# One 512-column matmul for both row parts in the second half of the keys, halves added by VectorE

## What is computed

```python
def step(ht):                                   # h: normed rows of the tokens
    q = (ht @ wq).reshape(T, 8, 2, 64)
    v1, i1 = lax.top_k(q[:, :, 0] @ keys1.T, 16)
    v2, i2 = lax.top_k(q[:, :, 1] @ keys2.T, 16)
    cv, ci = lax.top_k(v1[..., :, None] + v2[..., None, :], 16)   # over the 256 sums
    e = a * 128 + b                             # a, b: the two keys of a chosen pair
    g = jax.nn.softmax(cv, axis=-1)
    act = jax.nn.gelu(jnp.einsum('thkd,td->thk', u_tab[e], ht))
    return jnp.einsum('thk,thkd->td', (g * act), v_tab[e])
x = x + step(rms_norm(x, ffn_norm[l]))
```

## Time and profile before

| | |
|---|---|
| median of three runs | 2247.32 us (2244.87 to 2247.33) |
| the profiled execution | 2247.14 us |
| its span, first to last instruction | 2244.7 us |
| TensorE busy | 2190.7 us, 98% |
| weight loads | 1936.3 us, 86% |
| VectorE busy | 1182.9 us, 53% |
| ScalarE busy | 1169.5 us, 52% |
| GpSimd busy | 1742.0 us, 78% |
| mean granted TensorE clock | 0.991 of full speed |
| second half of the keys, layer 1 | from about 540 to 747 us |
| value pieces, layer 1 | from about 751 us on |
| second half of the keys, layer 2 | from about 1652 to 1860 us |

### The profile page before, as it was taken

One profiled execution on the slowest core, in us unless ns is written; L12 is line 12 of the kernel. 1 busy time (PEld: TensorE's weight loads), 2 busy tenths in 40 slices (PEclk: granted clock), 3 DMA queues, 4 the chain that ended last, 5 costly groups with the idle time before them and its releaser, 6 DMA issues.

```text
span 2244.7 us, 51285 instructions
## 1 busy us (share of the span) xinstructions
PE 2190.7 (98%) x15514; PEld 1936.3 (86%) x15514; DVE 1182.9 (53%) x2295; ACT 1169.5 (52%) x2277; POOL 1742.0 (78%) x1316
## 2 busy tenths in 40 slices
PE   7999999999999999999999999999999999999999
PEld 6887879999999888888879777799999998888887
DVE  5645447994343555434356455489744345554333
ACT  5445664555444444555553556645554444545565
POOL 6745957998777788888885567689987777888887
PEclk9999999999999999999998999999999999999999
DMA  7423534555444454465563334345544444545555
GB/s 265 151 94 113 169 114 149 178 168 170 160 165 160 155 166 167 168 210 191 189 242 122 105 121 160 124 158 174 170 162 163 159 164 154 166 167 188 196 188 177
DMA packets 100823, 368.20 MB, mean 164 GB/s; under 512 B 11520, under 2 KB 12032, under 8 KB 100480
## 3 DMA queue, kind: packets, MB, share of 16 engines
q1 hardware_dynamic: 97344, 354.46, 47.4%
q10 hardware_dynamic: 3392, 12.66, 1.5%
HBM read 366.03 MB, written 1.05 MB: 164 GB/s over the span
## 4 chain that ended last, share of the span: by engine, by line
PE 92%; issue 3%; DVE 3%; POOL 1%; ACT 1%; POOLq 0%; DVEq 0%
PE acc L1058 11%; PE acc L1141 11%; PE acc L1143 10%; PE acc L1142 10%; PE acc L1059 10%; PE acc L1060 10%; PE acc L838 6%; PE acc L840 6%; PE acc L839 6%; PE aux L1100 4%; PE aux L800 2%; POOL w_lo L458 1%; PE aux L951 1%; PE aux L974 1%; PE aux L886 1%
## 5 line engine op out<-in xcount | busy, mean ns | idle before, releaser
L458 POOL TENSOR_TENSOR w_lo<-raw,w_hi 128x512 fp32r<-128x512 f32 x1312 | 1741.8, 1342 | 493.1 <-ACT w_hi L489 385.2
L489 ACT ACTIVATE w_hi<-raw 128x512 fp32r<-128x512 f32 x1348 | 845.3, 629 | 807.8 <-PE acc L1060 419.6
L1058 PE MATMUL acc<-h_hi,w_hi 128*128 128x256 f32 x2048 | 587.3, 287 | 10.6 <-POOL w_lo L458 9.6
L1059 PE MATMUL acc<-h_lo,w_hi 128*128 128x256 f32 x2048 | 579.4, 283 | 0.0
L1060 PE MATMUL acc<-h_hi,w_lo 128*128 128x256 f32 x2048 | 579.1, 283 | 0.0
L1141 PE MATMUL acc<-w_hi,eg 128*128 128x512 f32 x1024 | 405.8, 396 | 0.0
L1058 PEld LDWEIGHTS acc<-h_hi,w_hi 128*128 128x128 f32 x2048 | 392.6, 192 | 14.1 <-POOL w_lo L458 12.5
L1143 PE MATMUL acc<-w_hi,eg 128*128 128x512 f32 x1024 | 399.5, 390 | 0.0
L1142 PE MATMUL acc<-w_lo,eg 128*128 128x512 f32 x1024 | 398.7, 389 | 0.0
L1059 PEld LDWEIGHTS acc<-h_lo,w_hi 128*128 128x128 f32 x2048 | 393.0, 192 | 0.1
L1060 PEld LDWEIGHTS acc<-h_hi,w_lo 128*128 128x128 f32 x2048 | 392.7, 192 | 0.0
(11 more groups left out here) (230 smaller groups left out, 2221.2 us busy)
## 6 DMA issues: line engine op xcount, KB each, us to landing
raw<-stream_dram SPq DMA_DIRECT2D x674, 512.0 KB, 3.3
big<-parb_dram ACTq DMA_DIRECT2D x2, 2128.0 KB, 10.6
big<-mem_dram ACTq DMA_DIRECT2D x3, 1024.0 KB, 5.1
big<-pm_dram ACTq DMA_DIRECT2D x2, 768.0 KB, 14.8
big<-parr_dram ACTq DMA_DIRECT2D x2, 640.0 KB, 12.7
X<-x_dram ACTq DMA_DIRECT2D x1, 1024.0 KB, 7.0
out_dram<-X SPq DMA_DIRECT2D x2, 512.0 KB, 2.9
big<-lnrow_dram ACTq DMA_DIRECT2D x2, 256.0 KB, 13.6
```

The source lines that it names most:

```text
L458: nc.gpsimd.tensor_tensor(w_lo[:, k % SLOTS, :], raw[:, k // PER_CHUNK, k % PER_CHUNK, :], w_hi[:, k % SLOTS, :].bitcast(F32), ALU.subtrac ...
L489: nc.scalar.activation(w_hi[:, k % SLOTS, :], raw[:, (k // PER_CHUNK) % RAW, k % PER_CHUNK, :], ACT.Copy).then_inc(hi_ready, 1)
L1058: pe_.matmul(dst, wh, h_hi[:, kt, :], start=(kt == 0), stop=False)
L1059: pe_.matmul(dst, wh, h_lo[:, kt, :], start=False, stop=False)
```

## The change

In the second half of the keys `h_hi` and `h_lo` lie side by side in one buffer `h_rows`, so that one matmul of 512 columns multiplies a block of high weights by both; its two products stand in the two halves of the bank. The low weights by the high rows are added to the first half as before (`key_both`). The new `key_sum` on VectorE adds the two halves and writes the sum to `experts`, and signals `u_sum`; ScalarE's gelu waits for that and works in place. VectorE does two `key_sum` in each period of its loop, behind `hot_weights`; the last four stand behind the loop. The first half of the keys stays with three matmuls. ScalarE's loop over the keys is cut in two at key 64.

At the turn, ScalarE does `key_hi` of keys 0 and 1 between its gelu of key 126 and the last two high parts of the key loop. VectorE does `weighted(0, 0)` ahead of the sum of key 127. TensorE's second gate step moves behind four value pieces (two keys).

```diff
--- before.py
+++ after.py
@@ -165,8 +165,8 @@
         w_hi = sb("w_hi", [P, SLOTS, COL], F32R)
         w_lo = sb("w_lo", [P, SLOTS, COL], F32R)
         X = sb("X", [P, T, D])
-        h_hi = sb("h_hi", [P, KD, S], F32R)
-        h_lo = sb("h_lo", [P, KD, S], F32R)
+        h_rows = sb("h_rows", [P, KD, 2, S], F32R)
+        h_hi, h_lo = h_rows[:, :, 0, :], h_rows[:, :, 1, :]
         big = sb("big", [P, BIG])
         eg = sb("eg", [P, 2, 2, S], F32R)
         cst = sb("cst", [P, K_END])
@@ -319,7 +319,7 @@
             xq_rows=1, xq_square=T,
             xq_mean=1, xq_sqrt=1, xs_ready=len(XUNITS), xo_ready=1,
             cv_ready=1, w_exp=1, w_ready=1,
-            u_out=KEYS, hot_a_made=2 * G_STEPS, hot_b_made=2 * G_STEPS, hot_w_made=2 * G_STEPS, g_full=2 * G_STEPS, g_out=2 * G_STEPS,
+            u_sum=KEYS - HALF, u_out=KEYS, hot_a_made=2 * G_STEPS, hot_b_made=2 * G_STEPS, hot_w_made=2 * G_STEPS, g_full=2 * G_STEPS, g_out=2 * G_STEPS,
             eg_hi=KEYS, eg_ready=KEYS,
             acc_free0=sum(v == 0 for v in PARITY.values()), acc_free1=sum(v == 1 for v in PARITY.values()))
         PRIMED = dict(layer_free=2, u_out=4, g_out=2, acc_free0=1, acc_free1=1)
@@ -683,13 +683,24 @@
 
                 def key_out(i, key):
 
-                    act.wait_ge(used, layer * PIECES + i * 8 + (PROJ + SLOTS + 2 * (key + 1)))
-                    nc.scalar.activation(key_rows(i, key), acc[:, (key + 2) % 4, 0:S],
-                                         ACT.Gelu_apprx_tanh).then_inc(sig["u_out"].sem, 1)
-
-                for k0, k1 in ((0, EXP_AT), (EXP_AT, KEYS)):
-
-                    a.step(nc.scalar.activation(tblw, tblw, ACT.Gelu_apprx_tanh))
+                    if key < HALF:
+                        act.wait_ge(used, layer * PIECES + i * 8 + (PROJ + SLOTS + 2 * (key + 1)))
+                        rows = acc[:, (key + 2) % 4, 0:S]
+                    else:
+                        act.wait_ge(sig["u_sum"].sem, layer * (KEYS - HALF) + i * 4 + (key + 1 - HALF))
+                        rows = key_rows(i, key)
+                    nc.scalar.activation(key_rows(i, key), rows, ACT.Gelu_apprx_tanh).then_inc(sig["u_out"].sem, 1)
+
+                def key_hi(i, key):
+
+                    if key >= 2:
+                        act.wait_ge(used, layer * PIECES + i * 8 + (SLOTS + PROJ + U_PIECES + 2 * (key - 1)))
+                    nc.scalar.activation(eg[:, key % 2, 0, :], key_rows(i, key), ACT.Copy).then_inc(sig["eg_hi"].sem, 1)
+
+                for k0, k1 in ((0, EXP_AT), (EXP_AT, HALF), (HALF, KEYS)):
+
+                    if k0 < HALF:
+                        a.step(nc.scalar.activation(tblw, tblw, ACT.Gelu_apprx_tanh))
                     if k0 == 0:
                         hi(2)
                     with act.Fori(0, (k1 - k0) // 4 - 1) as i:
@@ -702,7 +713,11 @@
                     done[0] += 2 * (k1 - k0) - 8
                     for q in range(4):
                         key_out(0, k1 - 4 + q)
-                        if k1 == EXP_AT or q < 3:
+                        if k1 == KEYS and q == 2:
+                            a.wait("g_out", G_STEPS)
+                            key_hi(0, 0)
+                            key_hi(0, 1)
+                        if k1 < KEYS or q < 3:
                             hi(2)
                     if k1 == EXP_AT:
                         a.wait("cv_ready")
@@ -710,15 +725,6 @@
                 sig["u_out"].sent += KEYS
 
 
-                def key_hi(i, key):
-
-                    act.wait_ge(used, layer * PIECES + i * 8 + (SLOTS + PROJ + U_PIECES + 2 * (key - 1)))
-                    nc.scalar.activation(eg[:, key % 2, 0, :], key_rows(i, key), ACT.Copy).then_inc(sig["eg_hi"].sem, 1)
-
-
-                a.wait("g_out", G_STEPS)
-                key_hi(0, 0)
-                key_hi(0, 1)
                 key = 2
                 for end in (HALF, LOAD_AT) + tuple(k + 2 for k in MEM_AT) + (KEYS,):
                     steps = (end - key) // 4
@@ -1060,6 +1066,17 @@
                     return pe_.matmul(dst, w_lo[:, r % SLOTS, wk * P:(wk + 1) * P], h_hi[:, kt, :],
                                       start=False, stop=(kt == KD - 1))
 
+                def key_both(r, kt):
+                    q, wk = r // 2, kt % 4
+                    bank_of, at = (q + 2) % 4, slice(wk * P, (wk + 1) * P)
+                    if kt:
+                        pe_.matmul(acc[:, bank_of, 0:S], w_lo[:, r % SLOTS, at], h_hi[:, kt, :], start=False, stop=False)
+                    ins = pe_.matmul(acc[:, bank_of, :], w_hi[:, r % SLOTS, at], h_rows[:, kt, :, :],
+                                     start=(kt == 0), stop=(kt == KD - 1))
+                    if kt == 0:
+                        ins = pe_.matmul(acc[:, bank_of, 0:S], w_lo[:, r % SLOTS, at], h_hi[:, kt, :], start=False, stop=False)
+                    return ins
+
                 def first_keys(k0):
                     for r in range(2 * k0, 2 * k0 + 4):
                         if r % 2 == 0:
@@ -1125,7 +1142,7 @@
                                 pe_.wait_ge(sig["u_out"].sem, layer * KEYS + i * 4 + (k0 + q + 1))
                             pe_.wait_ge(lo_ready, layer * PIECES + i * 8 + (HELD + PROJ + 2 * k0 + r + 1))
                             for k in range(4):
-                                ins = key_in(r, kh * 4 + k)
+                                ins = (key_both if k0 == HALF else key_in)(r, kh * 4 + k)
                             ins.then_inc(used, 1)
 
 
@@ -1143,9 +1160,9 @@
                         ins = pe_.matmul(dst, eg[:, q % 2, 1, ts], w_hi[:, slot, :], start=False, stop=stop)
                     ins.then_inc(used, 1)
 
-                weights_step(0, 0, 1)
-                weights_step(0, 1, 1)
                 for r in range(8):
+                    if r % 4 == 0:
+                        weights_step(0, r // 4, 1)
                     if r < 2:
                         pe_.wait_ge(sig["u_out"].sem, layer * KEYS + (KEYS + 3 + r))
                     value_piece(0, 0, r, start=r < 2)
@@ -1687,6 +1704,14 @@
                     V.tensor_tensor(v, v, aux[:, s % 2, :].rearrange("p (t a) -> p a t", t=G_TOK),
                                     ALU.mult).then_inc(sig["g_out"].sem, 1)
 
+                def key_sum(i, key):
+
+                    dve.wait_ge(used, layer * PIECES + i * 8 + (PROJ + SLOTS + 2 * (key + 1)))
+                    at = slice(key, key + 1) if isinstance(i, int) else bass.ds(i * 4 + key, 1)
+                    V.tensor_reduce(experts[:, at, :].rearrange("p o t -> p (o t)"),
+                                    acc[:, (key + 2) % 4, :].rearrange("p (n s) -> p s n", n=2),
+                                    AX.X, ALU.add).then_inc(sig["u_sum"].sem, 1)
+
                 def weighted(i, q):
 
                     src = experts[:, bass.ds(i * 4 + q, 1), :].rearrange("p o t -> p (o t)")
@@ -1706,16 +1731,23 @@
                         hot_rows(i, q + 1, 0)
                         weigh(i, q, 0)
                         hot_weights(i, q + 2, 0)
+                        for n in range(2):
+                            key_sum(i, HALF + 2 * q + n)
                 last = G_STEPS // 2 - 1
                 hot_rows(last, 1, 0)
                 weigh(last, 0, 0)
                 hot_weights(0, 0, 1)
+                for n in range(2):
+                    key_sum(0, KEYS - 4 + n)
                 hot_rows(0, 0, 1)
                 weigh(last, 1, 0)
                 hot_weights(0, 1, 1)
+                key_sum(0, KEYS - 2)
 
                 d.wait("g_out", G_STEPS)
                 weighted(0, 0)
+                key_sum(0, KEYS - 1)
+                sig["u_sum"].sent += KEYS - HALF
                 d.wait("u_out", KEYS)
                 d.settle()
                 with dve.Fori(0, G_STEPS // 2 - 1) as i:
```

## The result

The changed kernel takes 2228.31 us (median of four runs, 2227.8 to 2232.94) against 2246.16 us before on the same chip (2244.87 to 2247.33): a ratio of 0.9923, 95% interval 0.9911 to 0.9936, that is 17.3 us less (14.4 to 20.0). This gain and those of the experiments are the ratio times the time before, so they can differ by some tenths from the difference of the two medians (here 17.9). The profiled execution took 2227.8 us, its span 2226.0. Forecast: 2231.5, range 2226 to 2241.5, faster.

A forecast was written before the change was run, and what follows sets the result against it. The prediction took TensorE as the bound, each matmul costing its columns plus 13.3 ns, with a 2.28 us gap at each layer's turn. 2247.1 - 11.1 (pairs) - 4.6 (turn) = 2231.5 us, range 2226 to 2241.5.

The forecast's parts named there:

- Step 1, the pairs: Second half of keys: one 512-column matmul replaces two of 256; with the narrow one 0.3467 us, not 0.360; 11.1 us gained.
- Its columns and 13.3 ns, whatever its width: TensorE: each matmul costs its columns plus 13.3 ns at any width; 1024 fewer matmuls save 13.7 us before losses.
- The loss behind the gate step: Second half of keys: slower wide matmuls after each gate step lose 0.04 us a period, 2.6 us over 64 periods.
- Step 2, the sums: VectorE: 128 new `key_sum` reduces from PSUM take 0.69 us each, bounded at 1.2 us.
- No cost on the path: Second half of keys: the new VectorE sums hold nobody up and add nothing to the time.
- gone above 1.8 us a sum: VectorE in the second half of keys: the sums stay hidden until one takes over 1.8 us.
- Step 3, the turn: Turn from keys to values: reordering removes a 2.28 us gap in each layer, 4.6 us gained, at least 2.6.
- sum to 0.9, gelu to 1.3: At the turn, counted from the gate step's start: the last sum ends at 0.9 us, the last gelu at 1.3.
- The slack of 0.3 us: At the turn: `eg` of key 1 is ready at 3.0 to 3.2 us, due at 3.5; overrun up to 1 us a layer.
- A (pairs save less): Second half of keys: fewer matmuls save only 0 to 3 us, total 2239.5 to 2242.5 us; chance 0.13.
- B (a new wait at the turn): At the turn: late `eg` of key 1 or value piece 0 gives back 2 us, total 2233.5 to 2236; chance 0.10.
- C (VectorE as the bound): Second half of keys: VectorE sets the pace from 1.95 us a sum; at 2.3 us, total 2291 us; chance 0.06.

The follow-up runs named there:

- the turn alone: Changed kernel with three narrow matmuls in all keys and no sums, only the turn changed: 2239.51 us against 2246.2 before the change.
- everything but the width: Changed kernel with each wide matmul cut into two of 256 columns, sums and turn kept: 2240.89 us against 2246.2 before the change.
- the turn without its first half: Changed kernel with first `key_hi` behind the last gelu, `weighted(0, 0)` behind the last sum, second gate step still later: 2235.2 us against 2246.08 before.
- the experiment with two steps: Changed kernel with two extra VectorE steps ahead of each of the first 60 sums: 2229.69 us against 2246.08 before the change.

## Why the prediction was right, and where it was off

**The number.** 2231.5 was forecast and 2228.3 measured, within the range and 3.2 us under the forecast. The sum of the forecast was 11.1 + 4.6 = 15.7 us, and the traces show 11.5 + 4.1 = 15.6. So the terms were off by +0.4 and -0.5 and cancelled, which is luck; what is left of the difference is in stretches that the change doesn't touch. Over the three chips with this kernel the gain was 17.3, 16.2 and 18.2 us, each within 3 us by its interval.

**Step 1, the pairs.** Forecast 0.3467 a pair: measured 0.3467. "Its columns and 13.3 ns, whatever its width", read off two kinds of matmul that never stood side by side, holds for the mix in this execution; in others the keys of a layer ran at 0.353 a pair, which the forecast didn't have and which takes 2.1 us of a layer's 5.8. The loss behind the gate step was put at 0.04 us a period, two thirds of what the value stretch has: 16 x 0.3467 + 0.785 = 6.332, measured 6.364, so 0.03. The period forecast at 6.37 came out at 6.364. That this loss exists was read rightly, what makes it wasn't found; it isn't the gate step's own, for a mere wait has it too.

**Step 2, the sums.** Forecast 0.69 us, measured 692 ns at 256 results and a step of 256 elements, the two things that no row had. The Trainium skill ("SBUF — State Buffer", the part on cachelines) says that PSUM access patterns that aren't contiguous slow matmuls. It says so of matmuls, and VectorE's reads of PSUM show nothing like it: 677 ns in steps of 64 elements, 692 in steps of 256. "No cost on the path" is shown twice: the period with the sums and without the width is 6.544, as before, and one step more for each key costs nothing. The cover "gone above 1.8 us a sum" is borne out in the rough: with 1.8 us of queued work a key VectorE doesn't hold TensorE yet, with 2.4 the period grows by 1.06. Where between them it goes, no run shows.

**Step 3, the turn.** Forecast 4.6, measured 4.1. The 2.28 us went as described, in both layers, and a gate step behind no pause costs 0.14 less than the 0.86 it took there. One term was left out. The forecast has "sum to 0.9, gelu to 1.3" behind the gate step's start, and both came true: the sum ended at 741.38 (0.89) and the gelu at 741.83 (1.34). The step that failed is the next one, `hot_rows` right behind the gelu. It started at 742.36, 0.53 us after the gelu's end, for which the forecast had nothing. (With the turn alone it is 0.53 too, 748.43 to 748.96; what fills it isn't in the rows.) So `eg` of key 1 was ready at 3.49 and not at 3.0, which is the due time itself. The slack of 0.3 us was gone, and the piece came 0.16 us late. That wait and the slow spacings behind it are the 0.23 us by which the changed turn (12.77) is longer than the turn without the sums (12.54), where the gelu ends 0.24 us earlier and the piece isn't late. That is nearly all of what is missing in this term.

**The rivals.** A (pairs save less) is out by the spacings and by the kernel with everything but the width. The 2.5 ns that its paragraph quotes from the Trainium skill are given there for an isolated matmul; in these streams of matmuls, each with its weight load, it is 13.3. B (a new wait at the turn) came in the small: the forecast named this wait and its place, and gave it up to 1 us a layer; it was 0.16. In full it is what the turn without its first half shows, 1.8 us. C (VectorE as the bound) didn't happen, and its mechanism is real: 42.7 us slower than before when forced. Its own way in, a reduce at a fourth of the speed, found nothing in the trace of after. It was rightly given little.

**Where the forecast was blind.** The point from which C decides was worked out in durations. What counts on a full queue is the distance from start to start, 0.60 and not 0.69 us. At the change's own load this made no difference; in the experiment with two steps, 2254 us expected by durations and 2229.69 measured, it was nearly the whole miss.

## What to carry to other kernels

Where a matmul's spacing is its columns and a fixed part, count matmuls: two of 256 columns into one of 512 gave 13.3 ns each time at the usual pace, as long as the engine that must add the halves has the time, which is read from its start-to-start distances and not from its durations. A gap at a turn is the sum of late results, not of late instructions: list everyone who must be done before the next instruction, and move all of them or give the last one other work to hide behind, for one alone leaves nearly the whole wait (1.8 of 2.28 us). Look at a gain's own engine chain first: the same edit in a stretch where GpSimd makes the weights as fast as it can gave nothing clear. And before a small loss in one trace is put down to an edit, look for it in stretches that the edit leaves alone: the 0.07 us a period of the kernel with two extra steps stood in a kernel without them.

## What the runs showed of the hardware

- Queued VectorE steps that don't wait for one another overlap by 0.09 us: 0.69 in duration, 0.60 from start to start (700.28, 700.88, 701.48).
- The granted clock fell behind one pause of 1.82 us and not behind others of 1.79, 1.81 and 2.28 us. It came after the pause and cost 1.6 us, with seven spacings at 0.43. What sets the two apart isn't in these traces.
- After a break in a row of 512-column matmuls, a gate step of 24 or 8 matmuls or a bare wait of 0.16 us, about ten spacings are 0.231 or 0.232 us instead of 0.227, with VectorE at work or idle. Where all are of 256 columns, those behind the first are 0.118 to 0.120.
- A 512-column and a 256-column matmul in turn took 0.347 us a pair in most layers and 0.353 in others, with the same code and no wait: 6.364 or 6.433 us a period, one or the other for the whole of a layer's keys.
- A reduce out of PSUM costs by what it reads: 692 ns for 512 elements, whether it leaves 2 or 256 results, and whether its two operands lie side by side or 1 KB apart.
